# Reordering the copies, casts and block sums of a feed-forward stage, and starting it inside the stage before

## The reference

```python
x = x + jnp.einsum('bse,ed->bsd', y, w_out[l])          # output rows
h = rmsnorm(x, norm_ffn[l])
f = jax.nn.silu(jnp.einsum('bsd,df->bsf', h, w_gate[l])) * jnp.einsum('bsd,df->bsf', h, w_up[l])
x = x + jnp.einsum('bsf,fd->bsd', f, w_down[l])
return rmsnorm(x, norm_final)
```

## Time and profile before

| | |
|---|---|
| median of 3 runs | 2107.25 us (2106.31 to 2108.01) |
| profiled execution | 2107.95 us, of which the span in the trace is 2106.2 |
| PE | 94% busy, 8602 matmuls |
| DVE / ACT / POOL | 55% / 37% / 51% busy |
| granted TensorE clock, mean | 0.975 |
| DMA | 239 MB, 113 GB/s over the span |

### The profile page before, as it was taken

How to read it: one execution, slowest core, us unless ns; L and a number is a source line. 1 busy time by engine, 2 the same in 40 slices (tenths; PEclk the granted TensorE clock), 3 DMA queues, 4 the chain that set the end, 5 groups by cost and what they waited for, 6 DMA issues and landing times.

```text
span 2106.2 us, 23378 instructions
## 1 busy us (share of the span) xinstructions
PE 1975.9 (94%) x8602; PEld 1606.7 (76%) x8602; DVE 1155.1 (55%) x1205; ACT 783.4 (37%) x896; POOL 1063.9 (51%) x384
## 2 busy tenths in 40 slices
PE   6999899969998799999999899999998999999998
PEld 5887787847887677777777677777776888888886
DVE  5999899987546443434335433333341554574556
ACT  6366766674533432323324333232232111232112
POOL 2476559764524555655454445554544353443431
PEclk9999999979999899999999899999999999999999
DMA  5223222156675234323126232231237222252211
GB/s 157 60 71 107 83 92 69 60 200 203 215 243 158 85 114 143 112 90 103 61 70 199 74 97 65 70 105 60 70 101 301 98 100 100 80 199 80 100 59 80
DMA packets 213392, 238.60 MB, mean 113 GB/s; under 512 B 9902, under 2 KB 165550, under 8 KB 210010
## 3 DMA queue, kind: packets, MB, share of 16 engines
q1 hardware_dynamic: 213338, 237.89, 34.5%
HBM read 172.84 MB, written 65.01 MB: 113 GB/s over the span
## 4 chain that ended last, share of the span: by engine, by line
PE 72%; DVE 11%; issue 8%; POOL 4%; ACT 2%; DMA 2%; SPq 1%; DVEq 0%; ACTq 0%; POOLq 0%
PE ps L1716 17%; PE ps L1718 17%; PE ps L1717 17%; PE acc L1716 7%; PE acc L1718 6%; PE acc L1717 6%; DVE t_sum L1571 5%; DVE acc L1532 1%; DVE x L1694 1%; DVE x L1685 1%; PE ps L1741 1%; DVE wo_lo L1471 1%; POOL t_lo L815 1%; DVE gt L1605 1%; ACT p5s L1245 1%
## 5 line engine op out<-in xcount | busy, mean ns | idle before, releaser
L1532 DVE SCALAR_TENSOR_TENSOR acc<-glu,par,acc 128x1024 f32<-128x1024 f32 x232 | 298.9, 1288 | 7.2
L809 POOL TENSOR_TENSOR b_lo<-m_raw,b_hi 128x1536 fp32r<-128x1536 f32 x44 | 155.8, 3542 | 280.5 <-ACT b_hi L1171 280.5
L815 POOL TENSOR_TENSOR t_lo<-t_sum,t_hi 128x2048 fp32r<-128x2048 f32 x44 | 202.5, 4603 | 121.7 <-ACT t_hi L1176 121.7
L1685 DVE TENSOR_TENSOR x<-x,ps 128x512 f32<-128x512 f32 x264 | 179.5, 686 | 118.5 <-PE ps L1718 105.8
L876 POOL TENSOR_TENSOR f_lo<-f_raw,f_hi 128x2048 fp32r<-128x2048 f32 x22 | 102.3, 4648 | 255.2 <-ACT f_hi L1312 255.2
L1716 PE MATMUL ps<-wd_hi,f_hi 128*128 128x512 f32 x528 | 206.6, 391 | 7.6 <-POOL wd_lo L879 7.4
L1716 PE MATMUL ps<-h_hi,w_hi 128*128 128x512 f32 x512 | 203.2, 397 | 4.8 <-POOL w_lo L681 2.5
L1717 PE MATMUL ps<-wd_lo,f_hi 128*128 128x512 f32 x528 | 206.4, 391 | 0.0
L1718 PE MATMUL ps<-wd_hi,f_lo 128*128 128x512 f32 x528 | 206.2, 391 | 0.0
L1717 PE MATMUL ps<-h_lo,w_hi 128*128 128x512 f32 x512 | 200.8, 392 | 0.0
L1718 PE MATMUL ps<-h_hi,w_lo 128*128 128x512 f32 x512 | 200.8, 392 | 0.0
(11 more groups left out here) (208 smaller groups left out, 4623.3 us busy)
## 6 DMA issues: line engine op xcount, KB each, us to landing
m_raw<-in_w_gate SPq DMA_DIRECT2D x88, 256.0 KB, 4.1
m_raw<-in_w_up SPq DMA_DIRECT2D x88, 256.0 KB, 4.1
f_scr<-gt SPq DMA_DIRECT2D x88, 256.0 KB, 2.4
f_raw<-f_scr SPq DMA_DIRECT2D x22, 1024.0 KB, 4.8
wd_raw<-in_w_down SPq DMA_DIRECT2D x22, 1024.0 KB, 5.0
w_raw<-in_w_in SPq DMA_DIRECT2D x32, 512.0 KB, 5.3
xt<-in_x SPq DMA_DIRECT2D x16, 512.0 KB, 4.1
row<-in_x SPq DMA_DIRECT2D x16, 512.0 KB, 4.8
```

Source lines behind the costliest of these rows:

```text
L809: g.tensor_tensor(b_lo[b][:, :, :, :], m_raw[b][:, 0:3], f32(b_hi[b][:, :, :, :]), ALU.subtract).then_inc(s_mlo, 1)
L815: g.tensor_tensor(t_lo[b][:, :, :, :], t_sum[b][:, :, :, :], f32(t_hi[b][:, :, :, :]), ALU.subtract).then_inc(s_mlo, 1)
L1532: ins = v.scalar_tensor_tensor(out=into[:, :], in0=t[:, k:k + HALF], scalar=col(j, R_DW + k), in1=acc[:, :], op0=ALU.mult, op1=ALU.add)
L1685: v.tensor_tensor(x2[h][t][:, cols], x2[h][t][:, cols], ps[DOWN[bank]], ALU.add).then_inc(s_downf, 1)
```

## The change

The SBUF places of several tiles move, which is left out here: `t_hi[0]`, `t_lo[0]`, `t_sum[0]` go into the place of w_out chunks 0 to 3; `b_hi[1]`, `b_lo[1]`, `gt`, four of the `a_hi`, `f_hi[1]`, `wd_hi[1]`, and four `x2` tiles go elsewhere.

```diff
# SP, output rows
-                    for n, a in ((0, "A12"), (1, "A11"), (6, "A22"), (5, "A21")):
+                if LOAD_AT <= w < LOAD_AT + 2:
+                    for n, a in (((6, "A22"), (5, "A21")), ((1, "A11"), (0, "A12")))[w - LOAD_AT]:
                         sp_.dma_start(a_raw[n][:, :, :], quarter(0, a)).then_inc(s_a0, 16)
+                if w == LOAD_AT + 2:
                     load_matrix(0)
# SP, between the halves; store_quarter(n, ...) is one pass of the old loop in store_f
                         sp_.dma_start(a_raw[n][:, :, :], hs_scr[n - 2] if source is None else source
                                       ).then_inc(s_ald[n], 16)
+                        if n in (2, 4, 5):
+                            store_quarter((2, 4, 5).index(n), h, FI - 1, FI - 1)
+                    store_quarter(3, h, FI - 1, FI - 1)
...
-                store_f(h, FI - 1, FI - 1)
+                    store_f(h, FI - 1, FI - 1)
# POOL, output rows; the same three lines go behind row 15
+                if w == NT - 1:
+                    raw_lo(0, 0)
+                    pool.wait_ge(s_sum0, 4)
+                    a_low(0)
                 y_lo_part(w)
# POOL, up_block of the last matrix (f_low and wd_low are the halves of chunks_lo)
                 if not last:
                     raw_lo(m + 1, 0)
+                else:
+                    f_low(0, 0)
                 hidden(m, i, 0)
                 if not last:
                     sums_lo(m + 1, 0)
+                else:
+                    wd_low(0, 0)
# ACT, row 15
                 if w == NT - 1:
+                    act.wait_ge(s_sum0, 4)
+                    act.wait_ge(s_out[1], NT)
+                    a_high(2)
+                    sums_hi(0, 0)
                     row_std(w)
...
-            act.wait_ge(s_sum0, 4)
             act.wait_ge(s_out[3], NT)
-            a_high(2)
-            sums_hi(0, 0)
             a_high(3)
# ACT, gate_block
-                raw_hi(m + 1, 1, i + 1)
+                if starts is None:
+                    raw_hi(m + 1, 1, i + 1)
+                copy_p5(m, i, 0, first)
                 silu(i, 0)
-                if starts is None:
-                    sums_hi(m + 1, 1)
-                copy_p5(m, i, 0, first)
...
                 copy_u2(m, i, 0, first)
...
                 if starts is not None:
-                    sums_hi(m + 1, 1)
+                    raw_hi(m + 1, 1, i + 1)
+                sums_hi(m + 1, 1)
                 silu(i, 1)
# ACT, up_block
                 silu21(i, first)
-                if ends != 1:
-                    raw_hi(m + 1, 0, i + 2)
-                    sums_hi(m + 1, 0)
-                copy_p5(m, i, 1)
                 if ends == 0:
                     second_a_high(0)
-                copy_u2(m, i, 1)
-                if ends == 0:
-                    second_a_high(1)
-                    second_a_high(2)
                 if ends == 1:
                     chunks_hi(0, 0, 1, (s_pr[0], MATS), (s_pr[1], MATS))
                 else:
+                    raw_hi(m + 1, 0, i + 2)
+                copy_p5(m, i, 1)
+                if ends == 0:
+                    second_a_high(1)
+                copy_u2(m, i, 1)
+                if ends == 0:
+                    second_a_high(2)
+                if ends != 1:
+                    sums_hi(m + 1, 0)
                     copy_y(m + 1, i + 1, 0)
# DVE, row 15: add_row runs first_weight_sums between its two groups
+            def first_weight_sums():
+                for n in range(4):
+                    weight_sum(0, 0, n, 1)
...
+                    add_row(w, first_weight_sums if w == NT - 1 else None)
+                if w == NT - 1:
+                    a_low(0, 2)
                 dve.wait_ge(s_std2, w + 1)
# DVE, matrix_block
                         weight_sum(m + 1, 1 - b, 0, count)
-                        weight_sum(m + 1, 1 - b, 1)
                     if not b:
                         hidden21(i - 1)
-                    if not last:
-                        weight_sum(m + 1, 1 - b, 2)
                     sum11(m, i, b, first)
                     if not last:
-                        weight_sum(m + 1, 1 - b, 3)
+                        for n in range(1, 4):
+                            weight_sum(m + 1, 1 - b, n)
...
-            dve.wait_ge(s_out[3], NT)
-            for n in range(4):
-                weight_sum(0, 0, n, 1)
-            a_low(0, 2)
             a_low(0, 3)
```

More of the change, by code:

```diff
@@ L93, in hybrid_block @@
         a_raw = [at(f"a_raw{n}", [P, KH, TILE], F32, (64 + 8 * n) * KIB) for n in range(7)]
-        a_hi = [at(f"a_hi{n}", [P, KH, TILE], F32R, o * KIB) for n, o in enumerate((120, 128, 0, 8, 16, 24, 32))]
+        a_hi = [at(f"a_hi{n}", [P, KH, TILE], F32R, o * KIB) for n, o in enumerate((120, 128, 32, 40, 16, 24, 48))]
         m_raw = [at(f"m_raw{s}", [P, 4, KH, P], F32, o * KIB) for s, o in enumerate((184, 160))]
[L96 to L103, removed]
+        b_hi = [at(f"b_hi{s}", [P, 3, KH, P], F32R, o * KIB) for s, o in enumerate((192, 144))]
+        b_lo = [at(f"b_lo{s}", [P, 3, KH, P], F32R, o * KIB) for s, o in enumerate((198, 150))]
+        t_hi = [at(f"t_hi{s}", [P, 4, KH, P], F32R, o * KIB) for s, o in enumerate((0, 168))]
+        t_lo = [at(f"t_lo{s}", [P, 4, KH, P], F32R, o * KIB) for s, o in enumerate((8, 176))]
+        t_sum = [at(f"t_sum{s}", [P, 4, KH, P], F32, o * KIB) for s, o in enumerate((8, 176))]
+        gt = at("gt", [P, 2, HALF], F32, 56 * KIB)
+        y2s = at("y2s", [P, TILE], F32, 156 * KIB)
+        p5s = at("p5s", [P, TILE], F32, 158 * KIB)
         u2s = at("u2s", [P, TILE], F32, 216 * KIB)
@@ L107, in hybrid_block @@
         f_raw = [at(f"f_raw{s}", [P, 2, HALF], F32, o * KIB) for s, o in enumerate((136, 160))]
-        f_hi = [at(f"f_hi{s}", [P, 2, HALF], F32R, o * KIB) for s, o in enumerate((120, 0))]
+        f_hi = [at(f"f_hi{s}", [P, 2, HALF], F32R, o * KIB) for s, o in enumerate((120, 32))]
         f_lo = [at(f"f_lo{s}", [P, 2, HALF], F32R, o * KIB) for s, o in enumerate((64, 80))]
         wd_raw = [at(f"wd_raw{s}", [P, 2, D], F32, o * KIB) for s, o in enumerate((184, 208))]
-        wd_hi = [at(f"wd_hi{s}", [P, 2, D], F32R, o * KIB) for s, o in enumerate((128, 8))]
+        wd_hi = [at(f"wd_hi{s}", [P, 2, D], F32R, o * KIB) for s, o in enumerate((128, 40))]
         wd_lo = [at(f"wd_lo{s}", [P, 2, D], F32R, o * KIB) for s, o in enumerate((72, 88))]
-        x2_at = ((144, 148, 152, 156, 192, 196, 200, 204), (96, 100, 104, 108, 112, 116, 16, 20))
+        x2_at = ((0, 4, 8, 12, 192, 196, 200, 204), (96, 100, 104, 108, 112, 116, 16, 20))
         x2 = [[at(f"x2_{h}_{t}", [P, D], F32, o * KIB) for t, o in enumerate(row)] for h, row in enumerate(x2_at)]
@@ L564, in store_quad, with store_quarter @@
                     sp_.dma_start(hs_scr[n, :, k], quad[:, source]).then_inc(s_qst, 16)
-            def store_f(h, i, at_step):
[L568 to L574, removed]
+            def store_quarter(n, h, i, at_step):
+                step = FI * h + at_step
+                c, st, done = ((0, 0, (s_fm, 3 * step + 1)), (1, 0, (s_fm, 3 * step + 2)),
+                               (1, 1, (s_fm, 3 * step + 3)), (0, 1, (s_f21, step + 1)))[n]
+                cols = slice(st * TILE, (st + 1) * TILE)
+                sp_.wait_ge(*done)
+                sp_.dma_start(f_scr[h, i, :, c, cols].rearrange("a p s -> (a p) s") if not isinstance(i, int)
+                              else f_scr[h, i, :, c, cols], gt[:, c, cols]).then_inc(s_fst[n], 16)
+            def store_f(h, i, at_step):
+                for n in range(4):
+                    store_quarter(n, h, i, at_step)
             def next_matrices(h, i, at_step):
@@ L782, in y_lo_part, with raw_lo, sums_lo, a_low @@
                                 ALU.subtract).then_inc(s_ylo, 1)
+            def raw_lo(m, b):
+                pool.wait_ge(s_mhi, 2 * m + 1)
+                g.tensor_tensor(b_lo[b][:, :, :, :], m_raw[b][:, 0:3], f32(b_hi[b][:, :, :, :]), ALU.subtract
+                                ).then_inc(s_mlo, 1)
+            def sums_lo(m, b):
+                pool.wait_ge(s_mhi, 2 * m + 2)
+                g.tensor_tensor(t_lo[b][:, :, :, :], t_sum[b][:, :, :, :], f32(t_hi[b][:, :, :, :]), ALU.subtract
+                                ).then_inc(s_mlo, 1)
+            def a_low(n):
+                pool.wait_ge(s_ahi, n + 1)
+                g.tensor_tensor(a_lo[n][:, :, :], a_raw[n][:, :, :], f32(a_hi[n][:, :, :]), ALU.subtract
+                                ).then_inc(s_alo_pool, 1)
             gated_input(UNITS - 1)
@@ L804, in _ @@
                         fold(m, "cm")
-            def raw_lo(m, b):
-                pool.wait_ge(s_mhi, 2 * m + 1)
-                g.tensor_tensor(b_lo[b][:, :, :, :], m_raw[b][:, 0:3], f32(b_hi[b][:, :, :, :]), ALU.subtract
-                                ).then_inc(s_mlo, 1)
-            def sums_lo(m, b):
-                pool.wait_ge(s_mhi, 2 * m + 2)
```

(32 more changed lines are left out.)

## The result

| | before | after |
|---|---|---|
| median | 2107.63 us (4 runs, 2106.31 to 2110.81) | 2037.08 us (4 runs, 2033.8 to 2038.0) |
| profiled execution / its span | 2107.95 / 2106.2 us | 2033.8 / 2032.0 us |
| PE busy, granted clock | 94%, 0.975 | 96%, 0.982 |

The ratio is 0.9668, its 95% interval 0.9652 to 0.9684. The forecast was 2038.

A forecast was written before the change was run, and what follows sets the result against it. TensorE was taken to set the end from row 12 on, losing time to waits and the half clock after them. 53.7 + 1.8 + 3.9 + 9.9 = 69.3 us off 2107.95 gives 2038.6, stated as 2038; range 2028 to 2056.

The forecast's parts named there:

- Blocks, 53.7: Steady blocks of both halves: the `sum11` and p5 copy waits go, nothing replaces them; 30.5 + 23.2 = 53.7 us.
- rival B: Steady blocks: the p5 copy stays late, so 17 us stay and the result is 2055; chance 0.15.
- Rival E: Steady blocks: block sums start behind `b_lo`, `t_lo` slips and becomes the bound; slower, 2146; chance 0.03.
- Rows 13 to 15 and first matrix, 1.8: Row 13 gains 6.3 us, row 15 waits 7.8 and loses 2.4 more; net with first matrix 1.8 us.
- Between the halves, 3.9: Matrices 21 and 22: product 6 starts at 1176.3 against 1180.24, gaining 3.9 us; bounds 0 and 10.
- Down stage, 9.9: Ahead of the down stage: a 7.5 us wait and 2.4 us of half clock go, 9.9 us.
- The clock dip at 786: First half: clock 0.66 after a 2.08 us wait at 786.08; its loss was counted to that wait.
- 2041: Result if, by the skill page, this dip and a second in the first half stayed, 1.6 us each.
- The order at the port: VectorE and GpSimd's shared port: a waiting VectorE instruction goes next; if GpSimd went on unbroken, 1.2 us less.
- The total: Whole kernel: gains of 69.3 us take the profiled execution from 2107.95 to 2038.6; stated forecast 2038.

The follow-up runs named there:

- loops_only: The kernel before with only the new ScalarE order in the twenty-block loops and new VectorE order in all blocks but the first matrix's; 2054.68 us, 0.9753.
- u_dve: The changed kernel with VectorE's old order in the blocks (block sums 1 and 2 ahead of `sum11`), ScalarE's new order kept; 2059.31 us, 0.9782.
- u_act: The changed kernel with ScalarE's old order in the blocks (`t_hi` ahead of the p5 copy), VectorE's new order kept; 2174.11 us, 1.0326.
- u_spread: The changed kernel with the four operand loads in one go at row 10 again; 2041.79 us, 0.9693.
- ylo_first: The changed kernel with `y_lo(15)` put ahead of `b_lo` and `a_lo` 0 on GpSimd; 2033.51 us, 0.9654.
- mat1: The changed kernel with, in the first matrix, matrix 1's `b_hi` cast ahead of p5 and `a_lo` 6 made between `b_lo` and `t_lo`; 2026.7 us, 0.9621.

## Why the prediction was right, step by step

**Blocks, 53.7: right** (54.4 in the trace). loops_only shows the amount, u_dve and u_act show that both orders are needed. The rate of 0.2268 us a matmul from the down stage gave 381.1; it was 380.8. What wasn't seen is how the two orders lean on each other. The prediction priced a left-over p5 wait at 17 us (rival B) from the waits of before, where `t_hi` was early; with VectorE's new order and ScalarE's old one it is 139 (u_act). Rival E's mechanism, block sums late behind `b_lo`, is real, but in u_act what is late behind them is the p5 copy and not `t_lo`. The working of the blocks holds to 0.2 us: in the gate block above, `t_hi` starts 8.6 us and `t_lo` ends 15.3 us after product 6 of the matrix before, where 8.8 and 15.4 were said.

**Rows 13 to 15 and first matrix, 1.8: right** (1.9), and term by term. In the frame of before, 1.65 earlier, row 15 was to start at 666.3 and did at 666.2, after a wait of 8.0 where 7.8 was said. Twelve matmuls in the 5 us behind it instead of 22 are 2.3 us lost; 2.4 was said. Product 0 of matrix 1 waited 2.9 (3.3), product 6 started at 711.5 (711.0). u_spread and ylo_first undo one link each, mat1 undoes one and mends `a_lo` 6 with it.

**Between the halves, 3.9: mis-sized,** it was 6.2. The wait at product 3 is 3.5 us (4.3 said). Product 6 starts 44.96 us after the block of matrix 21 opens, where the working gave 46.4: 1.4 us. The working had `a_lo` 6 wait for `t_lo`, and it does, but `t_lo` ends 42.8 us after the opening, not 44.1:

```profile
1133.84 4.58 POOL L802 TENSOR_TENSOR t_lo<-t_sum,t_hi 128x2048 fp32r<-128x2048 f32 x1
1136.96 3.61 DVE L1569 TENSOR_TENSOR a_lo<-a_raw,a_hi 128x2048 fp32r<-128x2048 f32 x1 [2.50 <-ACT a_hi L1184]
```

And the half clock behind the last wait was shorter, 0.9 us less lost. In before and in after the stretch from product 6 to the next block reads:

```profile
1180.24:1185.24 5.00, 5.00 (x12) 3.94 (x13) 0.00 (x0) 0.00 (x0) 0.00 (x0) 0.50 0.00 0
```
```profile
1140.62:1145.26 4.64, 4.64 (x13) 3.74 (x14) 0.00 (x0) 0.00 (x0) 0.00 (x0) 0.63 0.00 0
```

The prediction took the two to be alike.

**Down stage, 9.9: right** (10.1). `f_lo` runs at 1528.53 and `wd_lo` at 1534.34, ahead of and between the quarters and no longer behind them:

```profile
1534.34 4.62 POOL L877 TENSOR_TENSOR wd_lo<-wd_raw,wd_hi 128x2048 fp32r<-128x2048 f32 x1
```

loops_only, with the old order there, keeps the wait of 7.4 us for `wd_lo` and takes 516.49. ScalarE's and GpSimd's parts of this edit were not run apart.

**The clock dip at 786.** It was counted to the wait of 2.08 us ahead of it. The wait went, and so did the dip: the clock is 1.00 over the whole stretch. A wait of that length doesn't always make a dip, though. Before has four waits for `sum11` of 2.1 us; the clock fell behind those that end at 786.08 and 912.23 (0.66 each) and not behind the two between:

```profile
828.99:833.99 5.00, 4.99 (x21) 3.82 (x22) 0.55 (x1) 3.55 (x4) 2.43 (x1) 1.00 1.01 284
870.59:875.59 5.00, 5.00 (x20) 3.78 (x21) 0.54 (x1) 3.56 (x4) 2.44 (x1) 1.00 0.98 280
```

The reading of the Trainium skill (TensorE: Matmul & The Clock Gate, Why this matters for your kernels) by which only longer gaps cost, and 2041 would result, did not hold here.

**The order at the port: wrong, without harm.** "A waiting VectorE instruction goes next" is true of one instruction only. With two on VectorE and more behind on GpSimd they take turns (7.61 us, and 3.19 once GpSimd had nothing to send). The sum didn't move, since its working never needed more: in the up block it let one block sum in behind `b_lo`, then `hidden` 0, then the other two, and that is the order in after. The Trainium skill (SBUF — State Buffer, Who interferes with whom) has whoever issues first hold the shared port for its whole instruction, and these traces agree (3.78 us in before for a block sum behind a `b_lo` of 3.50).

**The total.** The terms give 2038.6 for the profiled execution. It took 2033.8: 1.7 us in the stretch up to row 10, which isn't the change's, 2.3 between the halves, and 0.9 in small terms. It is the fastest of its four runs, 3.3 below their median. That the total is met within 1 us (2038 for 2037.08) is in part luck, and the terms are the better evidence.

## What to carry to other kernels

Put the instruction whose result a product waits for ahead of all that can be held up at a shared resource, on every engine of the chain at once: half of such an edit can cost more than it had to bring. Price the wait and the half clock behind it, and ask of every stall removed who is late next; at row 15 three quarters of a 10 us stall came back a few products later. An engine with queued work can be worth holding back for a moment when another has two short instructions to pass.

## What the hardware showed beside this

- With more than one instruction waiting on each side, VectorE and GpSimd took turns at their shared port, one whole instruction each: two block sums, 1.28 us when free, took 7.61 against two `a_lo` in a row, 3.19 against one.
- The half clock behind a wait isn't of one length. In 5 us, 12 matmuls ran after waits of 8.0 us (row 15) and 2.85 us (before, at 1180.24), but 15 after one of 3.5 us (1123.78); 22 is the full rate. Behind 2.1 us it was 15 or at least 20 (before, above). The length of the wait doesn't order them. What does was not tried.
- Waits of at most 2.9 us, once in every block, cost half as much again, mostly in clock (u_act): 11.9 us beside 21.4 of idle in 200. Read one by one in the two loops, the granted clock over the next 5 us was 0.50 to 0.71 behind 19 of 20 waits of 2.9 us, 3 of 4 of 2.2, and 1.00 behind the rest, among them all 16 of 1.5 or less. One of each:

```profile
1001.43:1006.43 5.00, 5.00 (x15) 3.94 (x16) 0.26 (x1) 0.43 (x1) 4.10 (x1) 0.66 0.00 0
1023.89:1028.89 5.00, 5.00 (x22) 4.15 (x23) 0.69 (x1) 1.07 (x2) 4.14 (x1) 1.00 0.57 162
```
